# A two-layer hybrid decoder trunk on one core: an unused tile of 1920 bytes in front of the weight rings

## What is computed

```
for layer in range(DEPTH):
    h = rms_norm(x, norm_w[layer])                     # 256 x 4096
    proj = einsum('bsd,de->bse', h, w_in[layer])       # 4096 x 11,792 weights
    split proj -> q/k/v/a of GLA, q/k/v of sliding window, q/k/v of differential attention, r_x, gate
    y = concat([gla(...), swa(...), diff(...), rglru(...)])   # 4 x 1024 columns
    y = y * silu(gate)
    x = x + einsum('bse,ed->bsd', y, w_out[layer])     # 4096 x 4096 weights
```

## The kernel before, in words

| tile | bytes | what it holds |
|---|---|---|
| `act` (`A`) | 65,536 | activations [32 k-tiles, 2 halves, 256 positions], float32r; one k-tile is 2048 bytes |
| `act_T` (`F`) | 32,768 | the same activations before their split, and scratch of the mixers |
| `mix_Y` (`YB`) | 32,896 | the mixers' results, and the input x at the start |
| `w_raw` | 16,384 | ring of 4 slots of raw weights, two rows of 512 float32 (2 x 2048 bytes) each |
| `w_hi` | 16,384 | ring of 4 slots, the weights rounded to float32r |
| `w_lo` | 12,288 | ring of 3 slots, what the rounding left |
| `stage`, `wa` | 4,096 each | gate staging; 32 weight slices of 32 columns (128 bytes) each |
| `ident` and others, `mix` (`MIX`) | rest | constants, parameters, scratch of the mixers |

## Time and profile before

### The profile page before, as it was taken

The page is one execution under the profiler, slowest core; times in us unless marked ns, Lnnn a source line. Parts: engine busy times, 40 slices in busy tenths (PEclk is TensorE's granted clock), DMA queues, the critical chain, the costliest instruction groups (busy, mean ns, idle before and its releaser), DMA issues.

```text
span 3024.1 us, 37606 instructions
## 1 busy us (share of the span) xinstructions
PE 2984.7 (99%) x14857; PEld 2480.8 (82%) x14857; DVE 1606.0 (53%) x2120; ACT 1458.7 (48%) x2059; POOL 52.8 (2%) x107
## 2 busy tenths in 40 slices
PE   8999999999999999999999999999999999999999
PEld 6778898888887898877878788988888787987877
DVE  5445456555666446444554445555556664554444
ACT  5344445545556455444543434445455665553333
POOL 2000000000000000000000000000000000000000
PEclk9999999999999999999999999999999999999999
DMA  7565556666555666666656655566655555666664
GB/s 225 168 184 158 160 163 178 177 182 177 174 161 163 179 180 193 209 209 198 207 172 187 180 155 165 164 178 178 179 174 174 160 167 174 187 197 201 216 213 163
DMA packets 281889, 546.68 MB, mean 181 GB/s; under 512 B 17688, under 2 KB 21920, under 8 KB 281712
## 3 DMA queue, kind: packets, MB, share of 16 engines
q1 hardware_dynamic: 271472, 524.88, 57.6%
q0 software_dynamic: 5552, 17.26, 1.9%
q10 hardware_dynamic: 4688, 2.13, 0.3%
HBM read 535.81 MB, written 8.39 MB: 180 GB/s over the span
## 4 chain that ended last, share of the span: by engine, by line
PE 98%; DMA 1%; ACT 1%; issue 1%; DVE 0%; ACTq 0%; PEldq 0%; DVEq 0%
PE main L1139 92%; PE mixer L1139 5%; DMA w_raw<-in_w_in 1%; ACT L383 0%; PE mixer L1353 0%; PE mixer L1198 0%; ACT stage L383 0%; PE mixer L1293 0%; PE mixer L1333 0%; PE mixer L1186 0%; DMA mix<-in_norm_w 0%; PE mixer L1321 0%; PE mixer L1283 0%; PE mixer L1320 0%; DVE w_lo L690 0%
## 5 line engine op out<-in xcount | busy, mean ns | idle before, releaser
L1139 PE MATMUL main<-w_hi,act 128*128 128x512 f32 x6912 | 2238.7, 399 | 26.4 <-PE main L1139 13.2
L690 DVE TENSOR_TENSOR w_lo<-w_raw,w_hi 128x1024 fp32r<-128x1024 f32 x992 | 1213.8, 1225 | 1281.0 <-PE main L1139 1045.6
L376 ACT ACTIVATE w_hi<-w_raw 128x1024 fp32r<-128x1024 f32 x992 | 1044.5, 1059 | 1138.1 <-PE main L1139 1123.1
L1139 PEld LDWEIGHTS main<-w_hi,act 128*128 128x128 f32 x6912 | 1302.8, 188 | 343.4 <-issue 39.6
L1139 PE MATMUL main<-w_lo,act 128*128 128x512 f32 x3456 | 1364.3, 395 | 0.0
L1139 PEld LDWEIGHTS main<-w_lo,act 128*128 128x128 f32 x3456 | 652.3, 189 | 143.4
L1139 PE MATMUL main<-act,w_hi 128*128 128x256 f32 x2048 | 373.7, 283 | 3.5 <-PE main L1139 1.8
L1139 PEld LDWEIGHTS main<-act,w_hi 128*128 128x128 f32 x2048 | 316.8, 188 | 6.2 <-issue 5.8
L1139 PE MATMUL main<-act,w_lo 128*128 128x256 f32 x1024 | 288.2, 281 | 0.0
L1139 PEld LDWEIGHTS main<-act,w_lo 128*128 128x128 f32 x1024 | 192.9, 188 | 0.2
L670 DVE SCALAR_TENSOR_TENSOR act<-act_T,par,act 128x256 fp32r<-128x256 f32 x96 | 42.0, 480 | 2.8 <-ACT act L358 2.5
(11 more groups left out here) (250 smaller groups left out, 1126.4 us busy)
## 6 DMA issues: line engine op xcount, KB each, us to landing
w_raw<-in_w_in SPq DMA_DIRECT2D x736, 512.0 KB, 3.6
w_raw<-in_w_out SPq DMA_DIRECT2D x256, 512.0 KB, 3.6
out<-mix POOLq DMA_DIRECT2D x15, 512.0 KB, 3.3
mix<-in_x POOLq DMA_DIRECT2D x8, 512.0 KB, 5.9
mix<-out POOLq DMA_DIRECT2D x8, 512.0 KB, 5.8
mix_Y<-in_x SPq DMA_DIRECT2D x3, 1024.0 KB, 16.6
mix_Y<-in_x SPq DMA_DIRECT2D x2, 512.0 KB, 5.0
act_T<-in_lru_w_r ACTq DMA_DIRECT2D x16, 64.0 KB, 1.9
```

Source lines behind the costliest of these rows:

```text
L376: act.activation(w_hi[:, n % HI, :, :], w_raw[:, n % RAW, :, :], ACT.Copy).then_inc(w_hi_ready, 1)
L690: dve.tensor_tensor(w_lo[:, n % LO, :, :], w_raw[:, n % RAW, :, :], w_hi[:, n % HI, :, :].bitcast(F32), ALU.subtract).then_inc(w_lo_ready, 1)
L1139: return pe.matmul(out_, lhsT, rhs, start=start, stop=stop, skip_group_check=True)
```

## The change

One tile, `pad`, of 480 float32 (1920 bytes) per partition is allocated between `mix_Y` and `w_raw`. Nothing reads or writes it. From `act` to `w_raw` it is then 133,120 bytes, 65 x 2048, and so the rings, `stage` and `wa` begin at the same offset within 2 KB as `act`. All tiles behind `pad` move up by 1920 bytes; the distances among them stay, and so do those among `act`, `act_T` and `mix_Y`.

```diff
         A = sb("act", [P, KT, 2, SEQ], F32R)
         F = sb("act_T", [P, KT * SEQ])
         YB = sb("mix_Y", [P, 6 * BW + HEADS * (SEQ + 4)])
+        pad = sb("pad", [P, 480])
         w_raw = sb("w_raw", [P, RAW, KG, NC])
         w_hi = sb("w_hi", [P, HI, KG, NC], F32R)
         w_lo = sb("w_lo", [P, LO, KG, NC], F32R)
```

## The result

The changed kernel takes 2979.61 us (median; 2976.47 to 2980.84) where the kernel before takes 3026.85 in the same comparison: a ratio of 0.9842, with a 95% interval of 0.9825 to 0.9859. The profiled execution took 2979.48 us, of which 2977.7 are its span, 46.4 less than before.

The account below looks back on a forecast made before the run. TensorE's matmul pace was taken as the bound, busy 2984.7 of 3024.1 us. All three terms were put at nothing, so the forecast was the unchanged median, 3026.3 us, within 6 us at 0.77; range 3005 to 3036 at 0.90.

Parts of the forecast that it names:

- the sum of the pace (2779 us): TensorE's main matmuls: 10,368 straight at 232.8 ns and 3072 turned at 118.9 ns make 92% of the span.
- (2): ScalarE's and VectorE's operands, in splits and evacuations: no cost on the path, within 1 us either way.
- (3): Landing of the weights by DMA in the moved rings: 6.3 us of cover, so nothing, within 1 us either way.
- (1): Addresses of the main matmuls' moving rows and stationary slices: 10,368 + 3072 matmuls x 0, bounds -21 and +9 us.
- bullet on the relative offset: `rank`'s slices walk through offsets within 2 KB; pitches of 0.24 us near zero offset exclude great effects, to 10 ns.
- bullet on the load's size: `rank` loads 32 columns, not 128, and saves 2.0 of 19.5 ns: at most a small part from reads meeting.
- bullet on what is moved: Float32 matmuls of 256 columns take 213 ns, exactly the clock, so the excess belongs to streaming float32r.
- Rows at the same addresses differ by as much as those at different ones: Reason for taking zero: straight chunks at the same addresses already take 44.87 or 45.05 us.
- lower bound of -21 us: Main matmuls: `rank`'s 2.0 ns better pace, if all due to the offset, times 10,368 straight matmuls.
- small gain: Rival: the main matmuls' two reads meet a little; the change saves 21 us, giving 3005; chance 0.08.
- much faster one: Rival: the main matmuls' whole 239 us excess is a matter of addresses, giving 2787 to 2850; chance 0.04.
- collision: Rival: with bases alike, moving stream and next stationary load collide, some 8 ns a straight matmul, 83 us, giving 3109; chance 0.06.

Follow-up runs that it names:

- f1_small_128: Kernel before, straight chunks' stationary slices cut to 32 columns except the first k-tile's, rings still at offset 128: 3008.91 us, 230.8 ns a straight matmul.
- f2_small_0: Kernel before with the same cut to 32 columns, plus the change's 1920 bytes, so rings at offset 0: 3018.31 us, 231.5 ns a straight matmul.
- e1_front: Kernel before with the 1920 bytes in front of `act`: rings at the changed kernel's addresses, offset against `act` as before: 3027.01 us, ratio 1.0002.
- e2_both: Kernel before with 128 bytes in front of `act` and 1920 in front of the rings, so both begin alike: 2979.03 us, ratio 0.9844.
- g1_lo_only: Kernel before with 1920 bytes between `w_hi` and `w_lo`: low ring at offset 0, high ring at 128: 2989.75 us, ratio 0.9877.
- g2_split64: Kernel before with rings at offset 0 for straight chunks, slots 256 bytes longer, turned chunks' groups 64 bytes further in: 2966.70 us, ratio 0.9803.
- e3_raw_only: Kernel before with `w_raw` alone moved to begin like `act`, `w_hi` and `w_lo` keeping their offset: 3026.44 us, ratio 1.0003.

## Why the prediction was wrong

What bounds the kernel, the sum of the pace (2779 us) and the list of what the change can touch at all were right: the whole 46.4 us are in the pace of the main matmuls, and nothing else changed by 1 us. Parts (2) and (3) held: splits of 1059 and 1224 ns, a landing of 3.6 us, waits of 15.0 and 8.5 us. That the chunks run alike with and without DMA traffic held too.

The step that failed is the term of (1), 10,368 + 3072 matmuls x 0. It measured -5.0 ns for each straight matmul and +1.15 for each turned one. Over all distances from one main matmul to the next of its kind that is -49.5 and +3.4 us, together 46.1 of the span's 46.4. The step that led to zero was to read from `rank` that the relative offset is worth nothing.

- The bullet on the relative offset took `rank` as a stand-in, since its slices walk through every multiple of 128 bytes. With a period of 256 bytes these are only two places, 128 and 0 by turns, before and after alike. The mean of `rank` holds both in equal parts, and so it barely moves: 230.8 and 230.9 ns (layers 0 and 1) before, 229.9 and 231.0 after. One by one its matmuls do differ. In layer 0 of before, those whose own slice lies at 0, beside which one at 128 is loaded, take 233.7 ns and the others 227.8; after the change, where the places are exchanged, it is 231.3 and 228.5 ns. Those of k = 14 and 15 take 232 and 239 ns where the prediction read 0.24 us twice. It read in steps of 10 ns, for an effect of 5, and the text said so and then took zero all the same.
- The loads of `rank` are moreover of 32 columns, and f1_small_128 and f2_small_0 show that with such loads the offset is worth 0.7 ns on average and the wrong way.
- The bullet on the load's size concluded from a small difference (2.0 ns) that two reads hardly meet. f1_small_128 confirms the number, 1.7 ns, and refutes the conclusion: that the length of the load alone changes little does not say that its place changes little when it is long.
- The bullet on what is moved found 213 ns for float32, no excess. By their starts these matmuls are 215 to 216 ns apart: the excess is some 2 ns there, small but not nothing.
- "Rows at the same addresses differ by as much as those at different ones" had no piece at another offset to compare its 0.18 us with: the trace of before has no such straight chunk. The difference turned out to be 1.07 us. The lower bound of -21 us, which set the range, came from the same `rank` row and was no bound.
- The rivals: the small gain had the right place and too low a price. The much faster one named the excess of 19.5 ns, of which the best offset takes a quarter. The collision had the sign wrong: beginning alike is the quick case for straight chunks and the slow one for turned ones. The page SBUF — State Buffer of the Trainium skill, section Who interferes with whom, was weighed as agreeing. Its rule that TensorE never waits on anyone is about engines against each other; of TensorE's own two reads it says only that their ports are independent. Here the places of the two operands do act on each other: 232.5 against 227.5 ns in e1_front and e2_both.
- The page TensorE: Matmul & The Clock Gate of the Trainium skill, section Back-to-back issue gap, gives the pace that the prediction took from it for a matmul by itself, and a shorter one, some 131 ns, for a sustained stream. No run here shows either: the shortest steady pitch of a straight piece is 226.7 ns.

Shown: the offset between the rings and `act` decides, as e1_front and e2_both tell it from the rings' own addresses. It acts through the two operands of the matmuls: in g1_lo_only the pitch follows, matmul by matmul, the ring that was moved, and in g2_split64 only the turned chunks' rows are moved and only their pace changes. `w_raw` has no part (e3_raw_only). Not told apart is whether a matmul's moving row meets its own stationary slice or the next one, which is loaded beside it: the slices of `act` all begin alike within 512 bytes. Open is what in the memory has the period of 256 bytes, and what the some 14 ns are that remain over 213.3 in the quickest straight chunks. That the two reads disturb each other in rhythms fits everything seen, but only the starts of the matmuls were measured, not the reads.

## What to carry to other kernels

When TensorE is the bound and its pitch is some per cent above its columns at the granted clock, where the tiles lie is a tuning parameter of its own: try a few unused tiles of 32 to 224 bytes between the moving and the stationary operand, and read the pitch of each kind of matmul from pieces of the chain. Different shapes want different offsets, so give each its own, as g2_split64 does. A stand-in from the trace tells something only if it agrees in every size that might matter, the load's columns included, and if it is read in finer steps than the effect and one by one, since a mean can hold both cases in equal parts. Where it doesn't, the range has to reach the whole unexplained excess.

## What the runs showed of the hardware

- A float32r matmul of 512 columns with loads of 128 columns had a mean pitch of 227.5 to 234.2 ns, and one of 256 columns 115.5 to 119.9 ns (stretches at 113.3), by the offset of its operands within 256 bytes, at a granted clock of 1.00.
- Matmuls of one and the same offset are not evenly spaced: at 128 the distances run from 228 to 241 ns and repeat in sevens, at 0 all are 226 or 227 ns.
- A matmul with a shorter load beside it can take longer: 227.5 ns with 128 columns, 231.5 with 32, at offset 0 (the result's rows were cut along with the load).
- Turned matmuls at one and the same offset have two steady rhythms, 113.3 and 117.8 ns, and kept one until a mixer's matmuls or a wait came between.
- A third of the rows aligned brought some 3.5 of 5.0 ns; the matmul behind an aligned one is quicker too (228.4 ns against 232.4).
